# Routing of a mixture-of-experts layer, moved chunk by chunk into the output projection before it

## The chip, the core and the metric

The kernel runs on one core of a Trainium2 chip. Its engines are TensorE (PE, matrix products into PSUM), VectorE (DVE) and ScalarE (ACT) for elementwise work, GpSimd (POOL), which here mainly issues gathers and scatters, and SyncE (SP), which issues the other DMAs. They run side by side and wait for each other on semaphores. The metric is the device time of one execution in microseconds (us).

## The reference

One step of a decoder layer, all in float32. For 1024 prompt and 32 sample tokens (1056 rows, in 9 chunks of up to 128) three parallel mixers are computed and concatenated. What follows is the part around the change:

```
mix = concat(attn, pool, memo) @ w_o               # 1056 x 1024 by 1024 x 1024
h1  = layer_norm(2**0.25 * x + mix, ln1_g, ln1_b)
p1  = softmax(h1 @ w_r1 + b_r1)                    # 4 expert groups
l2  = h1 @ w_r2 + b_r2                             # 4 x 8 experts
top-1 group by p1; in it the top-2 of 8 experts by l2, weights w2 = softmax of these two
gate[expert] = p1[group] * w2[expert]
y  = sum over experts of gate * (silu(h1 @ w_gate) * (h1 @ w_up)) @ w_down
out = layer_norm(2**0.25 * h1 + y, ln2_g, ln2_b)
```

Each of the 1056 tokens thus goes to 2 of 32 experts, and each expert has 2 x 1024 x 256 weights for gate and up and 256 x 1024 for down: 3 MB that are used once.

## The kernel before, in words

Products of large matrices are done in three passes: each operand is split into a rounded part ("high", a copy by ScalarE) and the rest ("low", a subtraction by VectorE), and TensorE adds high x high, high x low and low x high. Every engine has a program of its own, written out in order, and the order on each is the order in the code.

Ahead of the place in question stand the input projection and attention. Then, chunk by chunk (`mix(c)`, 2 x 24 matmuls), TensorE computes the output projection into two PSUM buffers in turn. VectorE adds alpha * x to a chunk and takes its mean and variance; ScalarE takes the root and applies mean and scale in a pass over the chunk (L1074); VectorE multiplies by ln1_g and adds ln1_b in two more passes (`affine`, L1368 and L1369). TensorE then transposes the chunk (`h1_transposes`, eight transposes, L855), ScalarE copies that out of PSUM, and the `router` multiplies it by the 1024 x 36 routing weights. In iteration c of the loop stand mix(c), the transposes of chunk c-1 and the router of chunk c-2. `store_h1` writes each finished chunk to DRAM, from where it is gathered later.

Behind the loop VectorE does the routing for all nine chunks at once (L1390 to L1474): `first_max` picks the group and the two experts as one-hot tiles of 9 x 32 columns; running sums over chunks and a product with a triangle of ones (TensorE) give every pair of token and expert its place in the expert's list; gate values are computed (with two exponentials on ScalarE); and 18 matmuls of a one-hot 128 x 128 tile with 96 columns (token number, pair number, gate) put these in their places. From their sum come the indices `IDX` (semaphore s_idx).

GpSimd then gathers the tokens of expert 0 and of three more ahead. For each expert TensorE transposes the gathered tokens (L895), ScalarE and VectorE split them, `gate_up` makes 24 matmuls, SiLU and product follow, and `down` gives the result, which GpSimd scatters to DRAM. The second norm ends the kernel.

SP loads the weights: four buffers for gate and up (1 MB halves, L484) and five for down (L487). When the last projection is done it issues those of experts 0 to 3 and down up to 4. From then on each half waits until gate_up of four experts earlier has done with that half.

```
pe.wait_ge(s_idx, 1)
gather_transposes(0)
for e in range(NE):
    gate_up(e)
    if e + 1 < NE:
        gather_transposes(e + 1)
    if e:
        down(e - 1)
    active_transposes(e)
```

## Time and profile before

| | us |
|---|---|
| median of three runs | 999.72 |
| lowest, highest | 998.92, 1000.36 |
| the profiled execution | 1000.77 |
| its span, first to last instruction | 998.9 |
| PE busy in the span | 893.8 |
| DVE busy | 559.6 |
| ACT busy | 398.6 |
| mean granted TensorE clock | 0.951 of full speed |

Busy time overlaps between engines. A granted clock of 1.0 is 2.4 GHz and one of 0.5 is 1.2 GHz; a stretch that has both shows a value between. Times in rows count from the span's start. A line number such as L657 is that of the helper that records the instruction, so matmuls are told apart by the tiles that they read. A float32 matmul is two records in the trace.

### The profile page before, as it was taken

The page shows a single profiled execution, that of the slowest core. Times are in us where ns is not written, and L with a number is a line of the kernel's source. Part 1 is how long each engine was busy: PE and PEld are TensorE (multiplying, and loading weights), DVE is VectorE, ACT ScalarE, POOL GpSimd, SP SyncE. Part 2 cuts the span into 40 slices and gives each one's busy share as a digit, 9 for nine tenths or more (in the row PEclk, how much of TensorE's full clock was granted, in tenths as well). Part 3 has the DMA queues.
Part 4 walks back from the last instruction along what each step waited for, and adds up shares of the span by engine and source line. Part 5 has one row for each costly group of instructions (what it writes and reads, how often), then busy time and mean ns, then how long its engine had stood idle before and what let it go on. Part 6 is the DMA issues. An engine that isn't in the chain of part 4 may idle for free.

```text
span 998.9 us, 13187 instructions
## 1 busy us (share of the span) xinstructions
PE 893.8 (89%) x5108; PEld 640.3 (64%) x5108; DVE 559.6 (56%) x1018; ACT 398.6 (40%) x748; POOL 189.2 (19%) x85
## 2 busy tenths in 40 slices
PE   6999999987899999868999934999999999999944
PEld 6999879963555545446888633666666666666511
DVE  6202020038665665693644367677777777777438
ACT  5202020024455645473312213545455555555236
POOL 0000000050000000000000001164646464645200
PEclk9999999998999999997999965899999999999978
DMA  9999999197876857507732096699999999997276
GB/s 353 304 353 361 371 338 362 62 381 223 269 289 241 294 171 252 206 6 263 288 111 82 27 360 251 222 354 361 356 364 353 355 356 365 362 378 283 89 293 244
DMA packets 54847, 273.49 MB, mean 274 GB/s; under 512 B 13984, under 2 KB 16544, under 8 KB 39680
## 3 DMA queue, kind: packets, MB, share of 16 engines
q1 hardware_dynamic: 46016, 247.97, 68.8%
q0 software_dynamic: 8768, 24.66, 7.1%
q8 instruction: 42, 0.69, 0.3%
q14 instruction: 21, 0.17, 0.1%
HBM read 256.33 MB, written 95.30 MB: 352 GB/s over the span
## 4 chain that ended last, share of the span: by engine, by line
PE 82%; DVE 10%; ACT 3%; issue 2%; DMA 2%; SPq 0%; DVEq 0%; POOLq 0%; ACTq 0%
PE psum L657 74%; PE psum L716 4%; PE psum L895 2%; DVE back L1237 1%; ACT back L506 1%; DMA middle<-pair_d 1%; DVE stats L1222 1%; DVE back L1219 1%; PE psum L855 1%; ACT back L1004 1%; DVE front L1245 1%; DVE front L1247 1%; PE psum L918 1%; DVE back L506 0%; DVE wo_low L1352 0%
## 5 line engine op out<-in xcount | busy, mean ns | idle before, releaser
L1659 POOL DMA_INDIRECT pair_d<-front,back x32 | 134.7, 4210 | 152.4 <-DVE front L1501 152.4
L657 PE MATMUL psum<-back,front 128*64 128x128 f32 (+1 forms) x904 | 151.9, 361 | 5.3 <-ACT back L506 4.4
L657 PEld LDWEIGHTS psum<-back,front 128*64 128x64 f32 (+1 forms) x904 | 71.4, 148 | 61.1 <-issue 52.5
L657 PE MATMUL psum<-gu_high,xg_high 128*112 128x512 f32 x256 | 104.2, 407 | 2.1 <-DVE xg_low L1486 2.1
L657 PE MATMUL psum<-gu_high,xg_low 128*112 128x512 f32 x256 | 102.1, 399 | 0.0
L657 PE MATMUL psum<-x_high,w_high 128*128 128x352 f32 x288 | 94.3, 327 | 8.3 <-DVE w_low L377 8.3
L657 PE MATMUL psum<-gu_low,xg_high 128*112 128x512 f32 x256 | 101.4, 396 | 0.0
L657 PE MATMUL psum<-front 64*128 64x256 f32 (+5 forms) x376 | 87.7, 491 | 10.3 <-DVE stats L1219 10.1
L657 PE MATMUL psum<-x_low,w_high 128*128 128x352 f32 x288 | 93.6, 325 | 0.0
L657 PE MATMUL psum<-x_high,w_low 128*128 128x352 f32 x288 | 93.4, 324 | 0.0
L1501 DVE SCALAR_TENSOR_TENSOR front<-psum,back 112x512 f32<-112x512 f32 x64 | 45.1, 746 | 68.8 <-PE psum L657 68.8
L506 ACT COPY back<-psum 128x512 f32<-128x512 f32 (+1 forms) x88 | 46.9, 547 | 85.3 <-PE psum L716 85.2
L1481 DVE TENSOR_TENSOR gu_low<-back,gu_high 128x1024 fp32r<-128x1024 f32 x64 | 74.0, 1218 | 0.2 <-ACT gu_high L1095 0.2
L716 PE MATMUL psum<-consts,back 128*128 128x128 f32 x352 | 61.4, 295 | 12.9 <-DVE back L1237 12.9
L1163 DVE TENSOR_SCALAR front<-psum 128x352 f32<-128x352 f32 (+5 forms) x26 | 13.8, 532 | 101.1 <-PE psum L657 101.1
L1639 POOL MEMSET back<- 128x1024 f32 x2 | 1.8, 951 | 361.5 <-PE psum L657 361.5
L657 PEld LDWEIGHTS psum<-front 64*128 64x128 f32 (+2 forms) x376 | 39.7, 194 | 47.4 <-issue 32.2
L1109 ACT ACTIVATE front<-psum 112x256 f32<-112x256 f32 x32 | 12.3, 385 | 142.2 <-PE psum L657 142.2
L716 PEld LDWEIGHTS psum<-consts,back 128*128 128x128 f32 x352 | 38.2, 145 | 42.7 <-issue 38.8
L1095 ACT CAST gu_high<-back 128x1024 fp32r<-128x1024 f32 x64 | 62.8, 1055 | 3.6 <-DMA back<-w_gu 3.5
L657 PE MATMUL psum<-wo_high,cat_high 128*128 128x512 f32 (+1 forms) x144 | 58.2, 404 | 3.1 <-DVE cat_low L1357 3.1
L986 ACT ACTIVATE front<-psum 128x352 f32<-128x352 f32 (+4 forms) x25 | 11.6, 468 | 123.5 <-PE psum L657 123.5
(210 smaller groups left out, 1677.9 us busy)
## 6 DMA issues: line engine op xcount, KB each, us to landing
back<-w_gu SPq DMA_DIRECT2D x32, 1024.0 KB, 16.4
out_win_k_s<-cache_win_k SPq DMA_DIRECT2D x16, 2044.0 KB, 13.8
out_win_v_s<-cache_win_v SPq DMA_DIRECT2D x16, 2044.0 KB, 12.3
back<-w_down SPq DMA_DIRECT2D x25, 1024.0 KB, 16.8
front<-w_gu SPq DMA_DIRECT2D x16, 1024.0 KB, 13.3
middle<-w_gu SPq DMA_DIRECT2D x16, 1024.0 KB, 13.9
back<-winkT SPq DMA_DIRECT2D x8, 1792.0 KB, 7.4
back<-cache_win_v SPq DMA_DIRECT2D x8, 1024.0 KB, 7.5
```

What stands on the lines that cost most here:

```text
L506: return copy(PTB[n % 4].rearrange("p a b -> p (a b)")[:, 0:w], bank(4 + n % 2)[:, 0:w])
L657: return nc.tensor.matmul(out, lhsT, rhs, start=start, stop=stop, skip_group_check=True)
L716: last = nc.tensor.transpose(b[:, (2 * j + s) * P:(2 * j + s) * P + P], SP[(u % 3) * 2 + s][:, kb * P:kb * P + P], ident)
L855: last = nc.tensor.transpose(bank(4 + hf)[:, j * P:j * P + m], H1[0:m, c, k * P:k * P + P], ident[0:m, 0:m])
L895: last = nc.tensor.transpose(bank(hf)[:, j * P:j * P + CAP], XG[e % 5][0:CAP, k * P:k * P + P], ident[0:CAP, 0:CAP])
L986: proj_out(n, lambda to, src: nc.scalar.activation(to, src, ACT.Copy, scale=proj[n][4])).then_inc(s_pe_a, 1)
L1095: nc.scalar.copy(GUH[e % 2][:, k, :], GUF[e % 4][:, k, :]).then_inc(s_wh, 1)
L1109: nc.scalar.activation(SIL[e % 2][0:CAP, :], bank(2 + e % 2)[0:CAP, 0:DE], ACT.Silu).then_inc(s_sil, 1)
L1163: proj_out(n, lambda to, src: V_.tensor_scalar(to, src, proj[n][4], None, ALU.mult)).then_inc(s_pe_d, 1)
L1481: V_.tensor_tensor(GUL[e % 4][:, k, :], GUF[e % 4][:, k, :], GUH[e % 2][:, k, :].bitcast(F32), ALU.subtract).then_inc(s_wl, 1)
L1501: V_.scalar_tensor_tensor(YS[e % 2][0:CAP, h], bank(4 + n)[0:CAP, :], GS[0:CAP, e:e + 1], XG[e % 5][0:CAP, h], ALU.mult, ALU.add).then_inc ...
L1659: G.indirect_dma_start(pair_d, bass.IndirectOffsetOnAxis(ap=IDX[0:CAP, NE + e:NE + e + 1], axis=0), YS[e % 2][0:CAP, :], None, bounds_chec ...
```

## The change

- **First norm.** ScalarE's pass and its buffer go. VectorE adds in place, and makes the norm in two passes: (x - mean) * g and then * (1/std) + b, with a reciprocal between.
- **Projection.** `mix` is cut into its two halves of 24 matmuls. In iteration c stand the first half of chunk c, the transposes of chunk c-1, the second half of chunk c, the router of chunk c-1, and the rank matmuls of chunk c-2.
- **Routing.** `chosen(c)` (16 steps, a running sum, two products with token numbers) makes the one-hot tiles of one chunk, `placed(c)` its places and its two one-hot 128 x 128 tiles, all 18 of which are kept. `positions(c)` adds a chunk's tokens to the indices by two matmuls. In VectorE's loop chosen(c-1) and placed(c-2) follow the norm of chunk c.
- **Gates.** The indices wait for token numbers alone. The gate values come after them on VectorE, and `gates` on TensorE (2 matmuls for counts, 18 with the kept one-hot tiles) stands behind the first gather's transposes.
- **Loads.** The kept one-hot tiles lie in the buffer of w_down of expert 3, which is therefore loaded only when `gates` is done (s_gs).

```diff
+        OH = [at(48784 + P * n, P) for n in range(16)] + [at(8192 + P * n, P) for n in range(2)]
...
@@ -591,28 +600,29 @@
             for c in range(CH):
                 if c >= 2:
-                    sp.wait_ge(s_r, c - 1)
+                    sp.wait_ge(s_t, c - 1)
                 sp.dma_start(XR[c % 2][0:rows(c), :], I["x"][c * P:c * P + rows(c), :]).then_inc(s_x[c % 2], 16)
                 if COPIES_PROJ + COPIES_RING + c < len(copies):
                     copy_cache(COPIES_PROJ + COPIES_RING + c)
-                if c >= 3:
-                    store_h1(c - 3)
+                if c >= 2:
+                    store_h1(c - 2)
             sp.wait_ge(s_mix, CH)
             for half in range(2):
                 load_gu(sp, 0, half)
+            for c in range(CH - 2, CH):
+                store_h1(c)
             load_dn(sp, 0)
-            for c in range(CH - 3, CH):
-                store_h1(c)
             for e in (1, 2):
                 for half in range(2):
                     load_gu(sp, e, half)
                 load_dn(sp, e)
-            load_dn(sp, 3)
             sp.wait_ge(s_ht, 2 * CH)
             sp.wait_ge(s_h1d, 16 * CH)
             for half in range(2):
                 load_gu(sp, 3, half)
             load_dn(sp, 4)
+            sp.wait_ge(s_gs, 1)
+            load_dn(sp, 3)
@@ -829,20 +839,20 @@
             pe.wait_ge(s_OB, NU)
-            def mix(c):
-                if c >= 2:
+            def mix(c, n):
+                if n == 0 and c >= 2:
                     pe.wait_ge(s_r, c - 1)
                 m = rows(c)
                 pe.wait_ge(s_lo, len(splits) + KT + c + 1)
-                for n in range(2):
-                    o = PS[0:m, 1024 * (c % 2) + 512 * n:1024 * (c % 2) + 512 * n + 512]
-                    for k in range(KT):
-                        cat_h, cat_l = (t[:, k, :] for t in cat_parts(c)[1:])
-                        wo_h, wo_l = (t[:, 512 * n:512 * n + 512] for t in wo_parts(k)[1:])
-                        mm(o, cat_h, wo_h, k == 0, False)
-                        mm(o, cat_h, wo_l, False, False)
-                        last = mm(o, cat_l, wo_h, False, k == KT - 1)
-                last.then_inc(s_mix, 1)
+                o = PS[0:m, 1024 * (c % 2) + 512 * n:1024 * (c % 2) + 512 * n + 512]
+                for k in range(KT):
+                    cat_h, cat_l = (t[:, k, :] for t in cat_parts(c)[1:])
+                    wo_h, wo_l = (t[:, 512 * n:512 * n + 512] for t in wo_parts(k)[1:])
+                    mm(o, cat_h, wo_h, k == 0, False)
+                    mm(o, cat_h, wo_l, False, False)
+                    last = mm(o, cat_l, wo_h, False, k == KT - 1)
+                if n:
+                    last.then_inc(s_mix, 1)
...
+            def rank(c):
+                pe.wait_ge(s_M, c + 1)
+                m = rows(c)
+                if 1 <= c < CH - 1:
+                    pe.wait_ge(s_oh, 2 * c)
+                o = ranks(c)
+                mm(o, tri[0:m, 0:m], RM[c % 2][0:m, :], True, False)
+                mm(o, ones[:, 0:m], RMP[c % 3], False, True).then_inc(s_rank, 1)
+            def positions(c):
+                m = rows(c)
+                pe.wait_ge(s_oh, 2 * c + 1)
+                mm(bank(2)[:, 0:NE], OH[2 * c][0:m, :], RVT[0][0:m, c, :], c == 0, c == CH - 1)
+                pe.wait_ge(s_oh, 2 * c + 2)
+                mm(bank(2)[:, 0:2 * NE].rearrange("p (a e) -> p a e", a=2), OH[2 * c + 1][0:m, :],
+                   RVT[1][0:m, c, :].unsqueeze(1).broadcast_to([m, 2, NE]), False, c == CH - 1).then_inc(s_ohx, 1)
             for c in range(CH):
-                mix(c)
-                if c >= 1:
+                mix(c, 0)
+                if c:
                     h1_transposes(c - 1)
+                mix(c, 1)
+                if c:
+                    router(c - 1)
                 if c >= 2:
-                    router(c - 2)
+                    rank(c - 2)
+            pe.wait_ge(s_r, CH - 1)
+            for c in range(CH - 3):
+                positions(c)
             h1_transposes(CH - 1)
-            router(CH - 2)
             router(CH - 1)
...
+            rank(CH - 2)
+            positions(CH - 3)
+            rank(CH - 1)
+            positions(CH - 2)
+            positions(CH - 1)
+            def gates():
+                pe.wait_ge(s_gv, 1)
+                counts = bank(7)[:, CH * NE:CH * NE + NE]
+                mm(counts, ones, RMP[(CH - 1) % 3], True, False)
+                mm(counts, ones[0:SMP, :], RM[(CH - 1) % 2][0:SMP, :], False, True)
+                for c in range(CH):
+                    m = rows(c)
+                    for k in range(2):
+                        last = mm(bank(7)[:, 320:320 + NE], OH[2 * c + k][0:m, :], RVG[k][0:m, c, :],
+                                  c == 0 and k == 0, c == CH - 1 and k == 1)
+                last.then_inc(s_gs, 1)
@@ -930,6 +974,7 @@
             pe.wait_ge(s_idx, 1)
             gather_transposes(0)
+            gates()
             for e in range(NE):
                 gate_up(e)
...
                     act.wait_ge(s_ht, 2 * c + hf + 1)
-                    if c >= 2:
-                        act.wait_ge(s_rt, c - 1)
-                    nc.scalar.copy(H1T[c % 2][:, 4 * hf:4 * hf + 4, 0:m],
+                    if c >= 1:
+                        act.wait_ge(s_rt, c)
+                    nc.scalar.copy(H1T[:, 4 * hf:4 * hf + 4, 0:m],
                                    bank(4 + hf).rearrange("p (j n) -> p j n", j=4)[:, :, 0:m]).then_inc(s_hte, 1)
             for c in range(CH):
                 m = rows(c)
-                act.wait_ge(s_r, c + 1)
+                if c >= 1:
+                    h1t_copy(c - 1)
+                act.wait_ge(s_mv, c + 1)
                 nc.scalar.activation(MV[0:m, c, 2:3], MV[0:m, c, 1:2], ACT.Sqrt, bias=EPSC[0:m, :]).then_inc(s_std, 1)
-                act.wait_ge(s_nrm, c + 1)
-                nc.scalar.activation(H1[0:m, c, :], RB[c % 2][0:m, :], ACT.Identity, scale=MV[0:m, c, 2:3],
-                                     bias=MV[0:m, c, 3:4]).then_inc(s_z, 1)
                 if c + 2 < CH:
                     cat_rounded(c + 2)
-                if c >= 1:
-                    h1t_copy(c - 1)
             h1t_copy(CH - 1)
-            act.wait_ge(s_rx, 1)
-            nc.scalar.activation(RX1, RX1, ACT.Exp).then_inc(s_ra, 1)
-            act.wait_ge(s_rx, 2)
-            nc.scalar.activation(W2, W2, ACT.Exp).then_inc(s_ra, 1)
...
-            def affine(c):
-                h = H1[0:rows(c), c, :]
-                dve.wait_ge(s_z, c + 1)
+            def first_norm(c):
+                m = rows(c)
+                x, h = XR[c % 2][0:m, :], H1[0:m, c, :]
+                mu, std = MV[0:m, c, 0:1], MV[0:m, c, 2:3]
+                dve.wait_ge(s_mix, c + 1)
+                dve.wait_ge(s_x[c % 2], 16 * (c // 2 + 1))
+                V_.scalar_tensor_tensor(x, x, ALPHA, PS[0:m, 1024 * (c % 2):1024 * (c % 2) + 1024], ALU.mult, ALU.add).then_inc(s_r, 1)
+                dve.wait_ge(s_r, c + 1)
+                for hf in range(2):
+                    last = V_.bn_stats(BN[0:m, 0, 6 * hf:6 * hf + 6], x[:, 512 * hf:512 * hf + 512])
+                step(last)
+                V_.bn_aggr(MV[0:m, c, 0:2], BN[0:m, 0, :]).then_inc(s_mv, 1)
+                dve.wait_ge(s_mv, c + 1)
                 if c == 0:
                     dve.wait_ge(s_gb, 64)
-                step(V_.tensor_tensor(h, h, GB[0:rows(c), 0, :], ALU.mult))
-                V_.tensor_tensor(h, h, GB[0:rows(c), 1, :], ALU.add).then_inc(s_h1, 1)
+                V_.scalar_tensor_tensor(h, x, mu, GB[0:m, 0, :], ALU.subtract, ALU.mult).then_inc(s_t, 1)
+                dve.wait_ge(s_std, c + 1)
+                step(V_.reciprocal(std, std))
+                dve.wait_ge(s_t, c + 1)
+                V_.scalar_tensor_tensor(h, h, std, GB[0:m, 1, :], ALU.mult, ALU.add).then_inc(s_h1, 1)
+            def chosen(c):
+                dve.wait_ge(s_rt, c + 1)
+                lg = logits(c)
+                top, p, a, b = (x[0:m, c:c + 1] for x in (m1, p1, v1, v2))
+                lx, rl, rs, down_, g4 = (x[0:m, :] for x in (LX, RL, RS, DOWN, TOPG))
+                first, second = (RE[k][0:m, c, :] for k in range(2))
+                step(V_.tensor_tensor_reduce(L1[0:m, c, :], lg[:, 0:NG], RT[0:m, 0:NG], 1.0, -3e38, ALU.add, ALU.max, top))
+                step(V_.tensor_tensor(lx, lg[:, NG:36], RT[0:m, NG:36], ALU.add))
+                step(V_.scalar_tensor_tensor(g4, L1[0:m, c, :], top, down_[:, 0:NG], ALU.is_equal, ALU.mult))
+                step(V_.tensor_reduce(p, g4, AX.X, ALU.max))
+                step(V_.tensor_scalar(g4, g4, p, -MASKED, ALU.is_lt, ALU.mult))
+                step(V_.tensor_tensor(rl.rearrange("p (g e) -> p g e", g=NG), lx.rearrange("p (g e) -> p g e", g=NG),
+                                      g4.unsqueeze(2).broadcast_to([m, NG, EPG]), ALU.add))
+                step(V_.tensor_reduce(a, rl, AX.X, ALU.max))
+                step(V_.scalar_tensor_tensor(rs, rl, a, down_, ALU.is_equal, ALU.mult))
+                step(V_.tensor_reduce(p, rs, AX.X, ALU.max))
+                step(V_.tensor_scalar(first, rs, p, None, ALU.is_equal))
+                step(V_.scalar_tensor_tensor(rl, first, -2.0 * MASKED, rl, ALU.mult, ALU.add))
+                step(V_.tensor_reduce(b, rl, AX.X, ALU.max))
+                step(V_.scalar_tensor_tensor(rs, rl, b, down_, ALU.is_equal, ALU.mult))
+                step(V_.tensor_reduce(p, rs, AX.X, ALU.max))
+                step(V_.tensor_scalar(second, rs, p, None, ALU.is_equal))
+                V_.tensor_tensor(RM[c % 2][0:m, :], first, second, ALU.add).then_inc(s_M, 1)
+                if c + 1 < CH:
+                    dve.wait_ge(s_M, c + 1)
+                    step(V_.tensor_tensor(RMP[(c + 1) % 3], RMP[c % 3], RM[c % 2], ALU.add))
+                for k in range(2):
+                    V_.tensor_scalar(RVT[k][0:m, c, :], RE[k][0:m, c, :], tok1[0:m, c:c + 1], None, ALU.mult)
+            def placed(c):
+                m = rows(c)
+                dve.wait_ge(s_rank, c + 1)
+                for k in range(2):
+                    step(V_.tensor_tensor_reduce((LX, RS)[k][0:m, :], RE[k][0:m, c, :], ranks(c), 1.0, 0.0,
+                                                 ALU.mult, ALU.add, (r1, r2)[k][0:m, c:c + 1]))
+                for k in range(2):
+                    V_.tensor_scalar(OH[2 * c + k][0:m, :], iota[0:m, :], (r1, r2)[k][0:m, c:c + 1], None, ALU.is_equal).then_inc(s_oh, 1)
             for c in range(CH):
...
-                affine(c)
+                first_norm(c)
                 if c + 2 < CH:
                     cat_rest(c + 2)
...
+                if c >= 1:
+                    chosen(c - 1)
+                if c >= 2:
+                    placed(c - 2)
+            chosen(CH - 1)
+            placed(CH - 2)
+            placed(CH - 1)
...
+            dve.wait_ge(s_ohx, CH)
+            empty, pair = RS, RL
+            step(V_.tensor_scalar(empty, bank(2)[:, 0:NE], 0.0, 1e6, ALU.is_equal, ALU.mult))
+            V_.scalar_tensor_tensor(IDX[:, 0:NE], bank(2)[:, 0:NE], -1.0, empty, ALU.add, ALU.add).then_inc(s_idx, 1)
+            step(V_.tensor_tensor(L1, L1, wide(m1, NG), ALU.subtract))
             dve.sem_inc(s_rx, 1)
...
+            def gate_values():
...
+                for k in range(2):
+                    step(V_.tensor_tensor(RVG[k], RE[k], wide((v1, v2)[k], NE), ALU.mult))
+                dve.sem_inc(s_gv, 1)
@@ -1670,6 +1710,8 @@
             for e in range(NE):
                 if e + 3 < NE:
                     gather(e + 3)
+                if e == 1:
+                    await_(s_pair, 1)
                 if e:
                     await_(s_yd, 2 * e)
```

TensorE, from the last projection matmul to the first of gate_up(0), before. `wo_high` are the projection's, 128x36 and 32x36 the router's, 128x288 the ranks', 128x96 the one-hot matmuls, 128x112 the transposes of gathered tokens:

```order
L657 MATMUL psum<-wo_high,cat_low 32x512
L855 MATMUL psum<-consts,back 128x128 x8
L657 MATMUL psum<-front,back 128x36 x8
L855 MATMUL psum<-consts,back 128x32 x8
L657 MATMUL psum<-front 128x36 x8
L657 MATMUL psum<-front,back 32x36 x8
L657 MATMUL psum<-front,consts 128x288 x2
L657 MATMUL psum<-back,consts 128x32
L657 MATMUL psum<-front,back 128x96 x18
L895 MATMUL psum<-consts,back 128x112 x8
L657 MATMUL psum<-gu_high,xg_high 112x512
```

After, from the last projection matmul (stats,consts are ranks, 128x32 with 128x64 a pair of positions):

```order
L667 MATMUL psum<-wo_high,cat_low 32x512
L667 MATMUL psum<-front,back 128x36 x8
L667 MATMUL psum<-stats,consts 128x32 x2
L667 MATMUL psum<-front,back 128x32
L667 MATMUL psum<-front,back 128x64
```

And from the rank of the last chunk on to gate_up(0) (behind the transposes stand the counts and the 18 gate matmuls):

```order
L667 MATMUL psum<-stats,consts 32x32 x2
L667 MATMUL psum<-front,back 128x32
L667 MATMUL psum<-front,back 128x64
L667 MATMUL psum<-front 128x32
L667 MATMUL psum<-front 128x64
L939 MATMUL psum<-consts,back 128x112 x8
L667 MATMUL psum<-stats,consts 128x32 x2
L667 MATMUL psum<-front,back 128x32 x16
L667 MATMUL psum<-front 128x32 x2
L667 MATMUL psum<-gu_high,xg_high 112x512
```

What moved: the router of chunk 7 stands ahead of the last transposes instead of behind them, ranks and positions are in pairs per chunk, only four matmuls stand behind the last chunk's rank, and 20 small ones now stand between the transposes of expert 0 and its gate_up.

SP's queue from the first expert load on, before (w_gu in halves, front, middle and back are places in the buffer memory):

```order
L484 DMA front<-w_gu 128x2048 [waits s_mix]
L484 DMA front<-w_gu 128x2048
L487 DMA front<-w_down 128x2048
L590 DMA h_d<-back 128x1024 [waits s_h1] x2
L590 DMA h_d<-back 32x1024 [waits s_h1]
L484 DMA middle<-w_gu 128x2048 x2
L487 DMA back<-w_down 128x2048
L484 DMA back<-w_gu 128x2048 x2
L487 DMA back<-w_down 128x2048 x2
L484 DMA back<-w_gu 128x2048 [waits s_h1d,s_ht]
L484 DMA back<-w_gu 128x2048
L487 DMA back<-w_down 128x2048
```

After, from the second half of that load on:

```order
L483 DMA front<-w_gu 128x2048
L599 DMA h_d<-back 128x1024 [waits s_h1]
L599 DMA h_d<-back 32x1024 [waits s_h1]
L486 DMA front<-w_down 128x2048
L483 DMA middle<-w_gu 128x2048 x2
L486 DMA back<-w_down 128x2048
L483 DMA back<-w_gu 128x2048 x2
L486 DMA back<-w_down 128x2048
L483 DMA back<-w_gu 128x2048 [waits s_h1d,s_ht]
L483 DMA back<-w_gu 128x2048
L486 DMA back<-w_down 128x2048
L486 DMA back<-w_down 128x2048 [waits s_gs]
```

What moved: two h1 stores instead of three stand in it, right behind the first load, and w_down of expert 3, which stood behind that of expert 2, now stands behind that of expert 4 and waits for s_gs.

## Rows read from the trace of the kernel before

**Rows 1.** Chain of waits, 560 to 935: start us, us, what.

```profile
562.24 12.92 PE psum L657 x64
...
577.74 0.21 DVE stats L1382
...
609.85 5.34 PE psum L657 x24
...
617.76 0.21 DVE back L1473
...
619.10 4.25 DMA back<-h_d,back
...
626.48 8.34 PE psum L657 x24
...
647.20 5.58 PE psum L657 x24
...
932.38 3.44 PE psum L657 x8
```

**Rows 2.** Stretches: us, PE, PEld, DVE, ACT, POOL busy, PEclk, DMA share, GB/s.

```profile
575.20:613.30 38.10, 14.26 (x86) 13.16 (x85) 27.21 (x80) 12.29 (x17) 1.84 (x2) 0.57 0.98 388
...
650.00:912.00 262.00, 262.00 (x1110) 171.29 (x1110) 198.65 (x237) 140.80 (x209) 147.10 (x53) 1.00 0.99 360
580.00:581.00 1.00, 0.00 (x0) 0.00 (x0) 1.00 (x1) 0.85 (x2) 0.00 (x0) 0.90 1.02 434
614.00:615.00 1.00, 1.00 (x7) 1.00 (x6) 0.67 (x3) 0.00 (x0) 0.00 (x0) 0.54 0.02 8
```

**Rows 3.** Loads of w_gu (L484) issued in 630–650, then in 890–915.

```profile
DMA to landing us min/median/max: 5.0/5.9/7.2
...
DMA to landing us min/median/max: 24.5/24.8/24.9
```

**Rows 4.** TensorE in order of time: start us, us, line, operation, count.

```profile
574.99 1.04 PE L855 MATMUL psum<-consts,back 128*128 128x128 f32 x8
575.86 1.87 PE L657 MATMUL psum<-front,back 128*128 128x36 f32 x16
...
583.44 3.63 PE L657 MATMUL psum<-front 128*128 128x36 f32 x16
...
623.48 1.73 PE L895 MATMUL psum<-consts,back 112*128 112x112 f32 x8 [6.96 <-DMA back<-h_d,back]
```

**Rows 5.** VectorE by form, 456–626: count, busy us, mean ns, idle before.

```profile
L1377 DVE SCALAR_TENSOR_TENSOR back<-back,psum 128x1024 f32<-128x1024 f32 x8 | 9.8, 1221 | 46.0 <-PE psum L657 46.0
...
L1462 DVE TENSOR_SCALAR back<-consts,back 128x128 f32<-128x128 f32 x18 | 4.8, 286 | 1.7 <-PE psum L657 0.2
...
L1431 DVE TENSOR_TENSOR front<-front 128x32 f32<-128x32 f32 x8 | 1.5, 192 | 0.3
...
L1408 DVE TENSOR_TENSOR front<-front,back 128x288 f32<-128x288 f32 x2 | 0.9, 458 | 0.1
```

**Rows 6.** VectorE by form, 230–456: scalar operands and an accumulating reduction.

```profile
L1176 DVE SCALAR_TENSOR_TENSOR middle<-middle,consts,front 64x1008 f32<-64x1008 f32 x4 | 5.1, 1264 | 0.1
...
L1219 DVE DVE_READ_ACCUMULATOR2_ANT stats<- 128x1 f32 x54 | 4.5, 83 | 0.0
...
L1219 DVE CUSTOM_DVE_ANT_0 back<-psum,back 128x128 f32<-128x128 f32 x6 | 1.7, 283 | 0.0
...
L1265 DVE TENSOR_SCALAR middle<-psum,stats 128x32 f32<-128x32 f32 x1 | 0.2, 242 | 0.0
```

**Rows 7.** Gathers (tile h_d) issued in 618–640, then in 650–680.

```profile
DMA to landing us min/median/max: 4.1/5.0/6.4
...
DMA to landing us min/median/max: 7.2/9.8/11.5
```

**Rows 8.** ScalarE in order of time, near the last experts.

```profile
928.50 0.33 ACT L1115 COPY front<-psum 128x224 f32<-128x224 f32 x1
931.65 0.38 ACT L1109 ACTIVATE front<-psum 112x256 f32<-112x256 f32 x1 [2.82 <-PE psum L657]
```

173 lines of the change are left out of this document (56 added, 117 removed).

## The prediction

> **What bounds the kernel now.** I read the chain of waits first, then busy time by stretch, then single engines round the place that the change touches. In the chain [rows 1] the reader is to see that TensorE sets the pace on both sides of one gap. The last chunk of the output projection ends at 562.24 + 12.92 = 575.16, and gate_up of expert 0 begins at 626.48. The 51.3 us between them are a chain of short VectorE instructions (first norm of the last chunk, routing) up to the indices at 617.76 + 0.21 = 617.97, then the gather of expert 0 (issued at 619.10, 4.25 long), its transposes and the split of its tokens. Behind the gap every expert is again TensorE end to end, 24 gate_up matmuls in 5.58 plus the rest. So time taken out of the gap reaches the end, unless the weights can't follow. That is a real limit: the DMA engines are busy 0.98 of 575–613 and 0.99 of 650–912 [rows 2], and a weight's time from issue to landing grows from 5.9 us at the first reloaded experts to 24.8 at the last [rows 3]: the weights fall slowly behind TensorE.
>
> The sum is made in the profiled execution's own time, 1000.77 (the span of 998.9 and 1.9 round it); the median of the runs shown, 999.72, is 1.05 less.
>
> **TensorE in the projection.** A chunk takes 12.92 for its 48 projection and 8 router matmuls [rows 1] and 0.87 for 8 transposes (574.99 to 575.86); the router's eight, recorded as 16, take 1.8 of it, 0.226 for one at the full clock [rows 4]. New in an iteration are two rank matmuls of the same kind (float32, 128 weight columns, few moving columns): 0.45. The end of the last projection moves back by what now stands ahead of it: one more set of transposes 0.87, one more router 1.81, the ranks of chunks 0 to 5, 6 x 0.45 = 2.7. Sum 5.4, so it ends at 580.6 (call it M). The transposes and router of chunk 7 lay behind that end before, beside the last norm, and cost nothing; that cover is given up. Bounds for the ranks: nothing, if they slip in beside other weight loads, and twice the price, that of the half clock.
>
> **VectorE in the projection.** A plain 32-wide instruction takes 0.192 with some 0.03 of gap behind it, a 1024-wide one 1.22, a 128x128 one-hot 0.286 [rows 5]; with a per-partition scalar 0.242 and 1.26, and an accumulating reduction of width 128 takes 0.283 and 0.083 for its read [rows 6], so I take 0.28 for the narrow ones. The norm has its statistics 577.95 - 575.16 = 2.8 after the projection [rows 1]; two passes of 1.26 and a reciprocal of 0.17 (the square root lies beside the first pass) make 5.5. `chosen` has 16 waited steps: six with a scalar, one accumulating, nine plain, 6 x 0.24 + 0.28 + 9 x 0.19 = 3.4, with the gaps 3.9; the running sum and two token products make 4.5. `placed` has two accumulating steps and two one-hots, 1.2. With `cat_rest`, 1.2, that is 12.4 a chunk, beside 12.92 + 0.87 + 0.45 = 14.2 of TensorE: 1.8 to spare. TensorE wants the normed chunk one router, one rank and half a projection after the chunk's end, 7.8 later, and has it at 5.5. So I cost this work at nothing; without that cover it costs what the last rival says.
>
> **The tail behind M.** VectorE is the chain: last norm 5.5, `chosen(7)` 4.5, `placed(6)` 1.2, `chosen(8)` to its mask 3.9, its token products 0.5, `placed(7)` and `placed(8)` 2.4: the last one-hot at M + 18.0. The ranks lie beside it (chunk 8's is out before `placed(8)` is reached). Then the last position matmul at the half clock 0.45, and two instructions on PSUM 0.5: indices at M + 19 = 599.6 instead of 617.97. The gate arithmetic and the pair numbers, some 3.5 us, stand behind the indices now, beside the gather.
>
> **The gather.** It was issued 1.1 after the indices into idle DMA engines and took 4.25 [rows 1]. Now SP's queue holds the prefetch, some 14.8 MB in the 38.1 us from 575.2 at 388 GB/s [rows 2]. It starts at M, loses one h1 store and the w_down of expert 3 (1.6 MB), and ends near 580.6 + 34 = 614.6, so the gather at 600.7 meets a full queue. Before shows gathers of 4.1 to 6.4 with little beside them, and up to 11.5 with weights beside them and a scatter ahead in their own queue [rows 7]. Ends: 4.25 and 11.5. I take 7, nearest the 6.4 and the 7.2, since no scatter stands ahead. Landed at 607.7; the eight transposes at the half clock take 1.73 [rows 4], to 609.5.
>
> What "DMA: Bandwidth & Descriptors" of the Trainium skill says under "Queues, rings and completion order" bears on this: each DMA engine goes round the queues that have work, a packet at a time. By that the gather shares the engines and doesn't stand behind the whole prefetch. No run here yet shows a lone gather against a full weight queue.
>
> **Gates.** Between those transposes and gate_up(0) stand 20 small matmuls that were not there (the 18 one-hot matmuls stood ahead of the indices). One takes 3.63 / 8 = 0.45 at the half clock and 0.226 at the full [rows 4]. The granted clock fell in 580–581, TensorE having been idle since 577.7 [rows 2, 4], and rose in 614–615, in the one-hot run that began at 609.85 [rows 1, 2]. I let it rise as long after its work begins here, at 612.7: 7 gates at 0.45 and 13 at 0.226, done at 615.7. The token split, which ended 626.48 - 623.48 - 1.73 = 1.3 behind the transposes, is covered. gate_up(0) then runs at the full clock, 5.6 instead of 8.34 [rows 1]: done at 621.4, where before it was done at 634.82. **Gain 13.4.** All at the half clock, the gates take 9.0 and gate_up(0) its 8.34: 5.6 less gain.
>
> **The weights behind.** Expert 4's first load is issued half-way through gate_up(0), at 618.5. By then the queue has had the prefetch, to 614.6, five gathers (2112 pairs over 32 experts, 4 KB each: 0.27 MB, all five 3.5 us), to 618.1, and w_down of expert 3, held until the gates are done, 2.7 more: 620.8. The stream starts 2.3 behind, where before it had nothing ahead. Near the end ScalarE's copy behind its last rounding is done at 928.83, and TensorE takes it at 932.38 [rows 1, 8]: 3.5 to spare. So 2.3 is just borne. Each microsecond beyond 3.5 comes off the gain one for one, and a faster tail would be kept only by about one more.
>
> 1000.77 - 13.4 = 987.4, or 986.3 by the median; I say 987, the limits being nearer on the slow side.
>
> **Rivals.** *The weight stream binds.* If the 15.6 MB behind M move at 360 GB/s as in 650–912 rather than at 388 [rows 2], the queue is free at 580.6 + 43.3 = 623.9, 5.4 behind; 1.9 over the 3.5: 989. For it: busy 0.99 and growing landing times. Against: the 388 was measured in this very stretch.
>
> *The gather waits, or the clock stays half.* In strict order of issue the gather lands at 614.6, 6.9 later: 994. With gates and gate_up(0) at the half clock: 993. For the first, the row of 11.5; for the second, that the clock fell after little idling.
>
> *A faster tail.* A gather of 4.25 and ranks at nothing: 5.4 more, but the stream keeps it to the 1 that it can spare, or all of it if the prefetch, too, ends earlier: 982 to 986.
>
> *Slower than before: VectorE becomes the bound of the projection.* 87 routing instructions, many of them 288 wide, become some 210 narrow ones, 23 a chunk. If each costs x more than its row, a chunk takes 12.4 + 23x, and beyond 14.2 each of 8 chunks waits; the tail has 50 of them. Loss 8 (23x - 1.8) + 50x; it eats the 13.4 at x = 0.12. At x = 0.15 it is 21: 1007. At the 0.458 of a 288-wide one, x = 0.26, it is 46: 1033 [rows 5]. Against: the rows of width 32, 0.19 to 0.24.
>
> The Trainium skill, "VectorE: DVE Perf Modes", under "The TRN2 errata — SBUF-src ops pay a fixed extra latency per instruction", speaks for this rival: many small tiles pay that latency each time. The trace agrees: nine times the width costs 0.458 against 0.192. With none of the routing hidden, 5.7 on each of 8 chunks, the time would be 1033.
>
> That the change doesn't do what it says is excluded by the instruction order: two VectorE instructions stand between the last position matmul and the gather.
>
> **Chances.** Forecast, with its own range of 984 to 989: 0.62. Stream binds, 989 to 991: 0.13. Gather or clock, 991 to 996: 0.13. Faster tail, 981 to 984: 0.08. VectorE binds: 0.04, of which slower than before 0.03. A range of 982 to 994 leaves out the last, half of the one before it and the worst of gather and clock, some 0.12. A measurement of this kernel tells 0.2%, 2 us, from no change: faster 0.95, same 0.02, slower 0.03.
>
> **What would show it.** The projection ends near 580.6 with no idle TensorE in it (idle time at the transposes would show VectorE as the bound); the indices come 19 us behind that, the first gather lands 7 after its issue, the gates take 6 with the clock rising among them, gate_up(0) takes 5.6; at the end ScalarE waits longer for w_gu and TensorE doesn't. The forecast is wrong if TensorE idles more than 2 us in the projection, if the indices come after 604, or if gate_up waits for weights.

## The result: 994.1 us, 5.6 us (0.56%) faster, a little under half of the forecast gain

| | before | after |
|---|---|---|
| median of the runs side by side | 1000.19 | 994.13 |
| lowest, highest | 998.92, 1000.36 | 992.12, 996.02 |
| the profiled execution | 1000.77 | 994.26 |
| its span | 998.9 | 992.4 |

Ratio 0.9944, 95% interval 0.9931 to 0.9957. The forecast was 987.0, range 982 to 994; 994.13 lies just outside. The 5.6 are the ratio's, and the two medians differ by 6.1; the two profiled executions, compared below, differ by 6.5.

The chain of waits of the changed kernel round the gap (start, length, what), which answers to [rows 1]:

```profile
573.64 5.61 PE psum L667 x24
579.27 1.22 DVE back L1408
...
596.63 0.20 DVE stats L1486
596.85 0.20 DVE back L1487
...
598.13 10.43 DMA back<-h_d,back
...
608.70 1.73 PE psum L939 x8
610.43 16.51 PE psum L667 x64
...
629.12 5.80 PE psum L667 x24
...
955.77 9.88 PE psum L667 x16
```

The last projection ends at 573.64 + 5.61 = 579.25, the indices are there at 597.05 (before 617.97), and the first gather, issued at 598.13, takes 10.43 instead of 4.25. Behind its transposes stands one run of matmuls, 16.51 long: the 20 gate matmuls (40 of the 64 records) and gate_up(0). gate_up(1) starts at 629.12 (before 637.00), and from there each expert takes what it took. The indices come 20.9 earlier, gate_up(1) 7.9.

The same place on TensorE (start, length, line, shapes, count, idle time before and its releaser):

```profile
608.70 1.73 PE L939 MATMUL psum<-consts,back 112*128 112x112 f32 x8 [12.11 <-DMA back<-h_d,back]
610.22 1.06 PE L667 MATMUL psum<-stats,consts 128*128 128x32 f32 x4
611.22 7.04 PE L667 MATMUL psum<-front,back 128*128 128x32 f32 x32
618.18 1.06 PE L667 MATMUL psum<-front 32*128 32x32 f32 x4
619.17 0.77 PE L667 MATMUL psum<-gu_high,xg_high 128*112 128x512 f32 x1
```

The gates run from 610.2 to 619.2: 9.0 for 20 matmuls, recorded as 40, that is 0.45 for one to the last. The stretches (length; busy time and count of PE, weight loads, DVE, ACT, POOL; granted clock, DMA share, GB/s) say why, and answer to [rows 2]:

```profile
579.25:597.00 17.75, 13.03 (x88) 11.96 (x87) 15.00 (x67) 5.96 (x8) 1.84 (x2) 0.59 0.95 361
582.00:583.00 1.00, 1.00 (x9) 1.00 (x8) 0.96 (x2) 0.29 (x1) 0.00 (x0) 0.73 0.87 369
597.00:608.60 11.60, 0.00 (x0) 0.00 (x0) 7.56 (x18) 4.22 (x6) 7.75 (x8) 0.50 1.02 367
608.60:627.00 18.40, 18.30 (x75) 16.06 (x76) 5.79 (x6) 2.38 (x4) 0.00 (x0) 0.60 0.95 290
517.20:531.40 14.20, 14.20 (x78) 12.08 (x77) 11.04 (x34) 2.33 (x5) 0.00 (x0) 1.00 0.21 76
623.00:624.00 1.00, 1.00 (x5) 0.70 (x5) 0.00 (x0) 0.00 (x0) 0.00 (x0) 0.79 0.78 229
```

The clock falls in 582–583, where TensorE has been busy without a break since the projection, with router, rank and position matmuls of 32 to 64 columns. It stays at half, 1.2 GHz, through the gates and comes back only in 623–624, 4 into gate_up(0). The row of 517.20 is one chunk of the projection: TensorE busy 14.20 of 14.20, VectorE 11.04, so the routing there is hidden.

### The profile page after: what moved, and what is told of

Its sections match the earlier page's. It is cut to its first block, busy times and chain, and to the rows that moved or that the text cites. A ratio compares the mean times of both kernels' runs of the same rounds, so it can differ in the third digit from the quotient of the medians.

```text
span 992.4 us, 13499 instructions
## 1 busy us (share of the span) xinstructions
PE 902.3 (91%) x5178; PEld 649.0 (65%) x5178; DVE 578.0 (58%) x1178; ACT 387.9 (39%) x739; POOL 186.9 (19%) x85
## 4 chain that ended last, share of the span: by engine, by line
PE 82%; DVE 10%; ACT 3%; DMA 3%; issue 2%; SPq 0%; DVEq 0%; POOLq 0%; ACTq 0%
PE psum L667 75%; PE psum L726 4%; PE psum L939 2%; DVE back L1276 1%; DMA back<-h_d,back 1%; ACT back L510 1%; DVE back L1258 1%; DMA middle<-pair_d 1%; DVE stats L1261 1%; PE psum L865 1%; ACT back L1049 1%; DVE front L1284 1%; DVE front L1286 1%; PE psum L962 1%; DVE back L510 0%
## 5 line engine op out<-in xcount | busy, mean ns | idle before, releaser
L667 PE MATMUL psum<-front 64*128 64x256 f32 (+5 forms) x320 | 79.8, 521 | 10.8 <-DVE stats L1258 10.5
L667 PEld LDWEIGHTS psum<-front 64*128 64x128 f32 (+2 forms) x320 | 32.4, 190 | 47.9 <-issue 32.2
L667 PEld LDWEIGHTS psum<-x_high,w_high 128*128 128x128 f32 x288 | 54.7, 190 | 8.4 <-DVE w_low L376 8.3
## 6 DMA issues: line engine op xcount, KB each, us to landing
front<-w_gu SPq DMA_DIRECT2D x16, 1024.0 KB, 13.2
```

Of the source, the lines that this page charges most:

```text
L667: return nc.tensor.matmul(out, lhsT, rhs, start=start, stop=stop, skip_group_check=True)
```

## The experiments

My theory after the result: TensorE ran at half clock from the tail on, so the gates cost 9.0 on the path and gate_up(0) 7.8, and the gather took 10.4 because it met the prefetch of weights. The rival was the weight stream, which would give back whatever is won ahead of it. Each ratio is to runs of the kernel before made beside it. The table's last column, **gap**, is read from each profile: from the end of the last projection to the start of gate_up(1). It leaves out what varied between profiles for no cause that I found: that end lay at 577.9 to 581.0 (b3 apart), mostly with the same instructions ahead of it, and the final sums, the same sixteen matmuls in all, took 8.5 to 10.2.

| | median | ratio to before, interval | gap |
|---|---|---|---|
| before | 1000.19 | | 61.8 |
| changed | 994.13 | 0.9944 (0.9931–0.9957) | 49.9 |
| a1_gates_first | 988.21 | 0.9882 (0.9864–0.9900) | 43.3 |
| a2_gates_late | 991.51 | 0.9924 (0.9905–0.9943) | 45.6 |
| a3_hold | 996.04 | 0.9961 (0.9946–0.9975) | 50.0 |
| a4_warm | 991.78 | 0.9919 (0.9903–0.9935) | 47.8 |
| b1_warm_first | 987.00 | 0.9863 (0.9846–0.9879) | 42.3 |
| b2_hold2 | 988.29 | 0.9880 (0.9863–0.9896) | 43.4 |
| b3_passes | 1023.58 | 1.0233 (1.0216–1.0250) | 53.8 |
| b4_gate_values_first | 994.62 | 0.9944 (0.9927–0.9961) | 51.3 |
| c1_clock_held | 985.32 | 0.9852 (0.9837–0.9866) | 40.5 |
| c2_clock_held_tail | 988.87 | 0.9873 (0.9842–0.9905) | 48.8 |
| c3_hold_clock_late | 987.38 | 0.9869 (0.9853–0.9885) | 40.5 |
| c4_one_pass | 995.81 | 0.9958 (0.9943–0.9973) | 50.2 |
| d1_hold_down2 | 990.21 | one run | 47.9 |
| d2_hold_half2 | 987.96 | one run | 44.7 |
| e1_both | 993.17 | 0.9930 (0.9908–0.9952) | 49.1 |
| e2_both_bridged | 985.78 | 0.9859 (0.9842–0.9875) | 40.8 |

**a1_gates_first.**

```
-            gather_transposes(0)
             gates()
+            gather_transposes(0)
```

> The gate matmuls go ahead of the transposes of expert 0: TensorE is idle from the indices (597.0) to the landing of the gather (608.6), and the gate arithmetic is done at 600.6, so the 9.0 us of gate matmuls lie beside the gather. Theory (the gates at the half clock on the path were the failed step): gate_up(0) begins at 609.7 + 1.73 + 1.3 = 612.8 instead of 619.2, at the half clock for some part, ends 621 to 623 instead of 626.9; 988 to 990, 4 to 6 less than the changed kernel. Rival (the weight stream binds): the same start of gate_up(0), but waits for weights later; no less than 992. Rival (the clock owes nothing to the gates): all of gate_up(0) at half, ended at 624: 991.

TensorE's timeline:

```profile
602.40 1.17 PE L667 MATMUL psum<-stats,consts 128*128 128x32 f32 x4 [4.09 <-DVEq L1507]
...
611.46 1.75 PE L939 MATMUL psum<-consts,back 112*128 112x112 f32 x8
614.50 0.77 PE L667 MATMUL psum<-gu_high,xg_high 128*112 128x512 f32 x1 [1.28 <-DVE xg_low L1525]
```

The gates still take 9.1, but 6.6 of the gap is gone, 5.9 of the median. Where the gates stand is the largest single part of what I missed, and the weights followed (TensorE waited for none).

**a2_gates_late.**

```
             gather_transposes(0)
-            gates()
+            pe.wait_ge(s_pair, 1)
...
                     gather_transposes(e + 1)
+                if e == 0:
+                    gates()
```

(Two one-hot tiles move in memory, and the load of w_down of expert 3 goes behind those of expert 4.)

> The gate matmuls go behind gate_up(0) and the transposes of expert 1; the w_down load of expert 3, whose place in memory they share, goes behind the loads of expert 4. gate_up(0) begins at 611.7 (landing 608.6, transposes 1.73, token split 1.3). If the narrow gate matmuls don't lift the clock, gate_up(0) takes its 8.3 of before and more, up to 9.5; if they do, it would take longer still without them ahead (10.8, all half). The gates then cost 4.5 at the full clock, 2.2 of it in a wait that is there anyway. gate_up(1) begins at 611.7 + 9 + 0.9 + 4.5 = 626.1 instead of 629.1: 991, about 3 less than the changed kernel. Rival (weight stream binds): no less than 993.

From the chain of waits, gate_up(0), gates, gate_up(1):

```profile
611.60 7.47 PE psum L667 x24
...
619.84 4.74 PE psum L667 x40
624.92 7.11 PE psum L667 x24
```

Without gates ahead of it gate_up(0) takes 7.5, with them 7.8: the 9.0 of gates had brought the rise of the clock no nearer. The gates at the full clock cost 4.7, close to the 4.5 expected, but the clock fell behind them, without any idle time, and gate_up(1) took 7.1 instead of 5.8. Gap 4.2 shorter, median 2.6.

**a4_warm.**

```
+            pe.wait_ge(s_wh, 4)
+            for _ in range(28):
+                mm(bank(5), GUH[0][:, 0, 0:P], GUH[0][:, 0, :], True, True)
             pe.wait_ge(s_idx, 1)
             gather_transposes(0)
```

> 28 matmuls of 512 columns, whose result nobody reads, stand behind the last position matmul, beside the wait for the gather (597 to 608.6). Theory (half clock is what made gates and gate_up(0) long): the clock rises within them, gates take 4.5 to 5 instead of 9.0 and gate_up(0) 5.6 instead of 7.8: 6 to 7 less, 987 to 988. If the clock does not rise in them they last 12.6, to 609.4, and the time is 0.8 more: 995. Rival (the stream binds): the gates and gate_up(0) get short, but the gain is lost to waits for weights: 991 to 994.

Stretches: the wide matmuls, the start of the gates, the rest of them with most of gate_up(0):

```profile
597.00:603.00 6.00, 6.00 (x17) 4.71 (x17) 5.17 (x17) 4.22 (x6) 4.14 (x5) 0.56 1.00 423
609.00:610.00 1.00, 1.00 (x6) 1.00 (x7) 1.00 (x3) 0.98 (x2) 0.10 (x1) 0.52 1.04 315
610.00:622.00 12.00, 12.00 (x44) 10.39 (x45) 4.35 (x4) 0.36 (x1) 0.00 (x0) 0.50 0.99 320
```

The clock rose late in the first stretch and was lost again at 609, with 1.45 of idling and the first gates behind it. The gates took 8.4, gate_up(0) 8.4. So the median has a third of the expected gain, and of the 2.1 by which this profile's gap is shorter 1.6 are an earlier landing (27.7 behind the last projection instead of 29.3): lifting the clock ahead of narrow work didn't keep it.

**b1_warm_first and c1_clock_held.** The gates first as in a1, with the wide matmul `W` (the `mm` of a4) among them:

```
+            for _ in range(10): W
             gates()                  # b1: a W behind every second gate matmul
+            for _ in range(5): W     # c1 alone
             gather_transposes(0)
+            for _ in range(6): W     # c1 alone
```

> As a1_gates_first, and with wide matmuls (512 columns, result unread) to hold the clock: ten behind the last position matmul, while the gate arithmetic runs, and one behind every second gate matmul. Theory (wide matmuls lift and hold the clock, the narrow ones alone don't): the clock is full from some 5 to 6 us behind the first wide one, the gates and the eight wide ones among them end at 610 to 611.5, transposes take 0.9 instead of 1.73, gate_up(0) 5.6 instead of 7.5: 3 to 4 less than a1_gates_first, 984 to 986. Rival (the wide ones among the gates don't hold it): gate_up(0) again 7.5 or more, and the eight add 3.6 at the half clock to the gates: 988 to 991.

> As b1_warm_first, with five more wide matmuls between the gates and the transposes of expert 0 and six more in the 1.4 wait for the token split. In b1_warm_first the clock fell at 609.7, in the idle time round the landing, and gate_up(0) ran 8.1. Theory (the fall is what these waits without wide matmuls cost): gate_up(0) at the full clock, 5.6, gate_up(1) begins at 618 to 619 instead of 621.3: 984 to 985 by the median, 2 to 2.5 less than b1_warm_first. Rival (the stream binds from here): TensorE waits for weights behind expert 20, no gain over b1_warm_first's 987.

Stretches of b1 (gates; round the landing; gate_up(0)), then of c1 (gates; to the split; gate_up(0)):

```profile
600.00:607.30 7.30, 7.06 (x49) 6.19 (x48) 4.85 (x5) 1.28 (x2) 6.03 (x6) 1.00 1.03 361
609.00:610.00 1.00, 0.42 (x5) 0.21 (x3) 0.36 (x1) 0.93 (x2) 0.00 (x0) 0.73 1.11 344
610.85:616.00 5.15, 5.15 (x12) 3.78 (x13) 4.48 (x4) 0.49 (x1) 0.00 (x0) 0.50 1.04 305
```

```profile
603.00:609.00 6.00, 6.00 (x43) 5.38 (x42) 2.62 (x3) 0.00 (x0) 3.51 (x4) 1.00 1.02 308
609.00:612.00 3.00, 2.99 (x18) 2.20 (x16) 1.20 (x3) 1.75 (x3) 0.00 (x0) 1.00 1.04 317
612.00:617.60 5.60, 5.59 (x24) 4.25 (x25) 4.50 (x4) 0.50 (x1) 0.00 (x0) 1.00 1.02 307
```

In b1 the clock holds through the gates and falls in the idle time round the landing; b1 came out 1 slower than expected. In c1 that time is filled, the clock stays at 2.4 GHz, gate_up(0) takes 5.6, and 985.3 is the lowest median here. The stream didn't bind, TensorE waits for no weight; but ScalarE, which rounds the weights, waits 17.4 for them in all (1.7 in the changed kernel), so it isn't far off.

**c2_clock_held_tail.** Six more wide matmuls in the tail (`mm(bank(5), ident, CS[:, 0:512], True, True)`, three ahead of the last transposes, two and one ahead of the last two ranks).

> As c1_clock_held, and six 512-wide float32 matmuls, unread, in the three waits of TensorE between the last projection and the last ranks (2.8, 2.0 and 1.5 long), 0.85 each at the full clock. Theory (the tail is VectorE's chain; TensorE's share of it is the last position matmuls, 2.2 at the half clock): indices about 1 earlier; of that, as in b4_gate_values_first, less than half reaches the landing: 983.5 to 985. Rival (the wide ones are late and push the ranks back): 1 to 3 more, 986 to 988.

The six runs spread from 983.7 to 993.4. In the profiled one, 993.42, the clock was half from 584 on, full again from 590.7, and fell at 604.6, behind 1.57 of idling, among the same gates and wide matmuls that hold it in c1. I call it inconclusive on the tail; it shows that the trick is not safe.

**a3_hold, b2_hold2, d1_hold_down2, d2_hold_half2.** One line, `sp.wait_ge(s_gx[0], 16)` (the first gather has landed), at four places in SP's list: ahead of w_gu of expert 3 (a3), of w_gu of expert 2 (b2), of w_down of expert 2 (d1), of the second half of its w_gu (d2).

> The loads of w_gu of expert 3 and w_down of expert 4 wait until the first gather has landed. Theory (the gather is long because of the weights beside it): the gather takes 4.3 to 6 instead of 10.4, what is left of the first three experts' weights (9.4 MB at 388 GB/s from 575, to about 599) being nearly through; the start of gate_up(0) comes 4.5 to 6 earlier, 988 to 990. Rival (the stream binds): the held loads are 2.6 MB, 6.9 us of stream; what is lost of it while the gather runs, 4 to 5 us, comes back as waits for weights at the end of the experts: 992 to 995. Rival (the gather's own cost): it still takes over 9 and nothing changes: 994.

> The changed kernel with the weights of experts 2 and 3 and w_down of expert 4 held until the first gather has landed. The loads before that, 6.3 MB of weights and 0.64 MB of stores, are through at about 597, so the gather meets idle queues. Theory (the gather's 10.4 is the weights beside it): 4.3 to 6, gate_up(0) 4.5 to 6 earlier. If the stream has the slack for it, 988 to 990; rival (the stream binds): 6 us of it are lost and come back as waits of TensorE for weights, 992 to 996. Rival (the gather's own cost): over 9 still, 994.

> The changed kernel with w_down of expert 2 and all loads behind it held until the first gather has landed: 8.4 MB of weights and 0.64 MB of stores stand ahead of the gather, against 6.9 MB in all in b2_hold2 (4.3 from issue to landing), 10.1 in a3_hold (10.7) and 13.2 in the changed kernel (10.4). If the gather comes behind what was issued before it, up to some amount: what is ahead is through at 580.9 + 9.0 MB at 415 GB/s = 602.7, and the gather lands 4 later, at 606.7, 8.8 from its issue. If it shares the queues evenly with what is under way, it needs about as long as in a3_hold as long as there is other work: 10 or so.

> The same with the second half of w_gu of expert 2 held as well: 7.3 MB of weights and 0.64 MB of stores ahead, through at 580.9 + 8.0 MB at 415 GB/s = 600.1. If the gather comes behind what was issued before it, it lands near 604.1, 6.2 from its issue. If it shares evenly: 4.3 to 5, since the queues are idle 2 behind its issue.

The gather's line in the chains, in the order a3, b2, d1, d2:

```profile
598.31 10.68 DMA back<-h_d,back
```

```profile
597.81 4.32 DMA back<-h_d,back
```

```profile
596.98 7.87 DMA back<-h_d,back
```

```profile
596.75 4.81 DMA back<-h_d,back
```

With 6.9, 8.0, 9.0 and 10.1 MB issued ahead of it in its stretch the gather takes 4.3, 4.8, 7.9 and 10.7 (d1 and d2 are one run each): the weights in the queues make it long. The changed kernel has 13.2 ahead and 10.4 (8.8 to 11.0 in the other profiles with 13.2), so the last 3.1, issued 7 to 8 us before the gather, add nothing; why they don't stays open. a3, which holds these alone, came out at 996.0, above all of its forecasts. How the gather shares the queues isn't shown either: d1's 7.87 lies nearer to the order of issue (8.8 forecast) than to even sharing (10 or so), but d2's 4.81 is what sharing forecast (4.3 to 5) and not the order of issue (6.2). The Trainium skill ("DMA: Bandwidth & Descriptors", "Queues, rings and completion order") has each DMA engine go round its queues a packet at a time. The trace agrees in that the gather doesn't wait for all of the prefetch: it landed at 608.6, where strict order would have made it 614.6 by the prediction's sum.

In b2 ScalarE waits for weights at the end:

```profile
ACT gu_high L1133 <- DMA back<-w_gu: 11.8, 9, 3.4
```

(total, times, longest), and a w_gu load 29.2 long stands in its chain of waits: from gate_up(1) to the end of the last gate_up with the down product behind it, it is 309.2 instead of 308.0. In d2 nobody waits for weights.

**b4_gate_values_first and c4_one_pass.** Two parts of the change taken singly: the gate arithmetic moved back ahead of the indices (`gate_values()` and the exponentials before `dve.wait_ge(s_ohx, CH)`), and one 1024-wide pass more in each first norm.

```
+                for _ in range(1):
+                    step(V_.scalar_tensor_tensor(h, x, mu, GB[0:m, 0, :], ALU.subtract, ALU.mult))
```

> One part of the change undone: the gate arithmetic (with the two exponentials of ScalarE) stands ahead of the indices again, the gate matmuls stay where they are. Theory (it was worth its own length, since indices and gather are the chain): indices 3 to 3.6 later, 997 to 997.6. Rival (the gather waits for the prefetch and not for the indices): the gather lands when the prefetch lets it, less than 1 later: 995.

> The changed kernel with one more 1024-wide pass in every first norm, as many passes as the norm had before. Theory (the projection has 2 of slack a chunk for it, the tail none): indices 1.3 later and 0.5 to 1.3 more at the end: 994.6 to 995.4. Without cover: 9 x 1.3 = 11.7 more, 1006.

```profile
600.00 9.38 DMA back<-h_d,back
```

```profile
599.20 9.09 DMA back<-h_d,back
```

In b4 the gather leaves 1.75 later (counted from the last projection) and is 1.05 shorter, in c4 1.3 later and 1.3 shorter. The landing moves by 0.7 and by nothing, the gap by 1.4 and 0.3, the medians by 0.5 and 1.7, with intervals that overlap the changed kernel's: on their own these two parts are worth little here. That the prefetch and not the indices decides when the gather lands is not shown by this. With the same tail, loads and gather (changed, a1, a2, a4, b1, c1) the landing lay 27.7 to 29.9 behind the last projection, and b4 has 30.0, c4 29.3; the indices of b4 came 1.75 later and not the 3 to 3.6 of the theory; and in c4 the longer norm also holds up the last store and the loads behind it, by 1.3.

**b3_passes.** As c4, three passes more (`range(3)`).

> The changed kernel with three more 1024-wide passes in every first norm, 3 x 1.28 = 3.8 of VectorE a chunk. The trace shows VectorE idle 2.35 in a chunk of 14.2. Theory (the narrow routing work is hidden while it fits): 1.5 more for each of some 7 chunks and all 3.8 in the tail, 13 to 16 more than the changed kernel: 1007 to 1010. If none of VectorE's work in the projection were hidden: 9 x 3.8 = 34 more, 1028. If there were ample cover: 3.8 more, 998.

The chain of one chunk, from the end of a half projection to the next, and the stretch of one chunk:

```profile
548.16 5.55 PE psum L667 x24
...
559.19 1.30 DVE back L1418
...
561.91 1.30 DVE back L1423
...
564.34 5.55 PE psum L667 x24
```

```profile
531.97:548.16 16.19, 14.41 (x78) 12.00 (x77) 14.90 (x39) 2.31 (x5) 0.00 (x0) 1.00 0.20 64
```

A chunk takes 16.19 instead of 14.20, since TensorE now waits for the norm: 9.5 of norm, 1.09 of transposes and 5.55 of half a projection stand in a ring. That is 2.0 a chunk, not 1.5; at the first two chunks TensorE's waits brought the clock down (a half projection 7.40 and 6.82 instead of 5.6). The last projection ends 23.0 later, the gap is 3.9 longer: here gather and loads both leave 3.9 later, and the landing comes 3.4 later. The cover is real and ends at about 2 a chunk; the price beyond it I set too low by half.

**c3_hold_clock_late.** b2's wait, the gates behind gate_up(0) as in a2 with `W` behind every second, 16 and 6 `W` in the waits before.

> The weights of experts 2 and 3 held until the first gather has landed (as b2_hold2), the gates behind gate_up(0) with a wide matmul behind every second one, and wide matmuls in the waits before gate_up(0). TensorE's part alone: gate_up(0) from 604.4 to 610, gates to 617, gate_up(1) from 617.5 instead of 622.3, and the kernel 4.8 less than b2_hold2: 983.5. Rival (the weight stream, which in b2_hold2 already cost 1.2 behind expert 20, sets the end): no gain or under 1.5 over b2_hold2: 987 to 988.5, with TensorE waiting for w_gu at the end.

```profile
ACT gu_high L1143 <- DMA back<-w_gu: 24.2, 12, 3.6
```

```profile
PE psum L669 <- ACT front L1163: 2.1, 2, 1.3
```

(Total, times, longest: ScalarE waits for weights, and TensorE for ScalarE.) gate_up(1) starts as early as in c1, but from there to the end of the last gate_up with the down product behind it, it is 310.8 instead of 308.0: here the stream takes back 2.8. The rival is real, but only where the prefetch is delayed.

**e1_both and e2_both_bridged.** d2's wait and `W` in the changed kernel's own order: 12 `W` ahead of the landing in e1, 24 in e2, one behind every second gate matmul in both.

> Both causes taken away at once, with the order of the changed kernel kept: the second half of w_gu of expert 2 and all behind it held until the first gather has landed (d2_hold_half2: 4.8 to landing, no wait for weights at the end), twelve wide matmuls behind the last position matmul and one behind every second gate matmul (c1_clock_held). Seen from the changed kernel's start: landing 603, transposes 0.9 to 604, gates and eight wide ones at the full clock 6.4 to 610.4, gate_up(0) 5.6 to 616, gate_up(1) from 618.3 where c1_clock_held has it at 619.7: 983 to 985, if the stream follows. Rival (the stream sets the end, as in c3_hold_clock_late): 986 to 988. If the clock falls among the gates: gate_up(0) 7.5 to 8, 986 to 989.

> As e1_both with 24 wide matmuls instead of twelve behind the last position matmul, so that they reach to the landing. In e1_both TensorE idled 2.86 before it, the clock fell at 602.8 and came back only in gate_up(0). Theory (clock and gather are the two causes and add up): the clock stays up from the wide ones on; counted from the end of the last projection, landing 24, transposes 0.9, gates with eight wide ones 6.4, gate_up(0) 5.6, gate_up(1) begins 39 to 40 behind that end (61.8 before, 49.9 changed kernel, 40.5 c1_clock_held): 983 to 985. Rival (the stream sets the end): the same start, with waits for weights and 986 or more. If the clock falls among the gates again: 988 or more.

e1, stretches: the twelve, idle to the landing, transposes with gates, gate_up(0):

```profile
596.24:600.60 4.36, 4.36 (x13) 3.18 (x12) 3.47 (x16) 3.56 (x6) 2.44 (x3) 0.67 1.00 417
600.60:603.40 2.80, 0.01 (x1) 0.00 (x0) 2.80 (x3) 0.66 (x1) 2.36 (x3) 0.85 0.64 189
603.40:617.50 14.10, 14.03 (x56) 12.76 (x56) 7.45 (x8) 2.35 (x3) 2.95 (x3) 0.50 0.96 308
617.50:623.00 5.50, 5.50 (x14) 4.01 (x14) 0.00 (x0) 0.00 (x0) 0.00 (x0) 0.50 1.01 337
```

e2, chain of waits (the 24 with the last positions, transposes, gates with gate_up(0), gate_up(1)):

```profile
593.17 10.24 PE psum L669 x32
603.41 0.77 PE psum L943 x8
604.18 12.41 PE psum L669 x72
...
618.77 5.81 PE psum L669 x24
```

2.8 of idling cost e1 the clock, and with it nearly all the gain: 993.2 is above all of its forecasts, since at the half clock gates and wide matmuls took 12.5, 3.5 more than the gates alone. e2 closes that time, and gates, eight wide matmuls and gate_up(0) take 12.4. It is 14.1 faster than before (0.9859 of 999.87), 0.8 short of what was expected of it: with clock and gather both set right, a gain of the forecast's size (13.4) is there, in the changed kernel's own order on TensorE, at the price of 32 unread matmuls and held loads.

## Why the prediction was wrong, step by step

The mechanism was right: the routing is hidden in the projection and the gap shrinks. Two terms of the sum were mis-sized, and both stand behind the indices: the gather, and above all the clock of the gates and of gate_up(0) behind them.

- **M:** the last projection ends at 579.25, forecast 580.6. From the first norm of chunk 0 it lies 5.85 later than before (111.1 from 468.13, against 105.3 from 469.89), forecast 5.4; it began 1.76 earlier, within the spread of the profiles here.
- **VectorE hidden:** right, at 11.04 of 14.20 (forecast 12.4); b3 shows where it ends.
- **Tail:** indices 17.8 behind M, forecast 19. Whether the landing follows a small shift of them is open (b4, c4).
- **"I take 7" for the gather:** 10.43, inside my bounds of 4.25 and 11.5 but 3.4 over. I had set it near gathers that met few weights; here it met queues full of weights, and with these held it takes 4.3 (b2).
- **"I let it rise as long after its work begins here, at 612.7":** the step that failed most. The rise at 614–615 before stood in a run of one-hot matmuls [rows 2], and I moved it with the work, as if the gates were the same work. They aren't: a one-hot matmul had 96 columns before and has 32 here (row below). The clock rose in 623–624, so the gates took 9.0 and not 6.2, and gate_up(0) 7.8 and not 5.7: 4.9 together. a1, c1 and e2 show that this is where the time lies.
- **The weights behind:** right for the changed kernel, and in c1 down to a gap of 40.5; c3 shows the limit where loads are held.

The run of one-hot matmuls of before, in whose course the clock rose:

```profile
609.85 6.67 PE L657 MATMUL psum<-front,back 128*128 128x96 f32 x36 [5.19 <-DVE back L1462]
```

The rows of before that were nearest to the gates spoke against me: the router's matmuls of 36 columns, with transposes ahead of them, kept TensorE busy for 5.7 without a break from 582.45 on, and the granted clock was 0.50 throughout. One stretch of them:

```profile
585.00:586.00 1.00, 1.00 (x6) 1.00 (x7) 0.00 (x0) 0.12 (x1) 0.00 (x0) 0.50 0.93 381
```

That the columns are the reason is not shown: no run changes them alone.

The sum, from the last projection to the end of gate_up(0): forecast 40.8, measured 47.7 = 40.8 - 1.2 (tail) + 3.4 (gather) + 2.8 (gates) + 2.1 (gate_up(0)) - 0.2 (rest). M gave 1.35 back, and the final sums took 9.88 instead of 8.53, for which I had nothing: 6.9 - 1.35 + 1.35 = 6.9 over 987.4, the profiled 994.26.

My rival "the gather waits, or the clock stays half" comes nearest, but not as I had it. Its first half put the landing at 614.6, in strict order of issue, and had 994 from that alone; the landing came at 608.6. Its second half had 993; the gates took all of its 9.0, gate_up(0) 7.8 of its 8.34. A part of the one and most of the other came together, and that the sum is again 994 is chance. I gave the rival 0.13 by treating the two as alternatives of one small chance, and by letting a single rise of the clock in the trace of before, in wider matmuls, stand for a rule.

## What to carry to other kernels

When work leaves TensorE's shadow, price what then stands between idle time and the next large matmuls at the half clock, at both ends, and look first whether it can lie beside the wait instead of behind it: swapping two lines (a1) was worth as much as the whole change. Before a measured rise or fall of the clock is carried to other work, check that the matmuls are of the same shape. A transfer that starts earlier can meet what is still in the queues; ask what is already issued when it is (10.4 here, 4.3 in b2). A held clock can be bought with unread wide matmuls (c1, e2), but a short idle stretch can lose it and the gain with it (2.8 in e1, 1.57 in the profiled run of c2).
